# Two stacked transformer blocks in one kernel: the order of work around the last stick-breaking units of block one

## What is computed

```python
def hybrid_layer(x, ...):
    h = rmsnorm(x, g_pre) @ w_in
    (a_q, a_k, a_v, b_b, b_c, b_x, c_q, c_kv, c_kr, d_q, d_k, d_v, gate) = jnp.split(h, SPLIT_IDX, axis=-1)
    ya = swa_sink_attention(...)          # 4 heads, window 128
    yb = short_gated_conv(b_b, b_c, b_x, conv_w, conv_b)
    yc = mla(...)                         # 4 heads, latent attention
    yd = stick_breaking_attention(...)    # 4 heads
    y = jnp.stack([ya, yb, yc, yd], axis=2)
    y = rmsnorm(y, g_grp.reshape(N_GROUPS, GROUP_WIDTH)).reshape(b, s, D_MIX)
    y = y * jax.nn.silu(gate)
    return x + rmsnorm(y @ w_out, g_post)

def stick_breaking_attention(q, k, v):    # per block of 128 queries
    z = q k^T * scale
    log_keep = where(mask, log_sigmoid(-z), 0)
    after = cumsum(log_keep, reverse=True) - log_keep
    a = where(mask, exp(log_sigmoid(z) + after), 0)
    return a @ v
```

## Time and profile before

| quantity | value |
|---|---|
| median of 3 runs | 2416.64 us |
| lowest and highest of them | 2414.21, 2417.61 us |
| the profiled execution's own time | 2422.64 us |
| its span, first to last instruction | 2420.8 us |
| mean granted TensorE clock | 0.982 |
| PE busy | 2270.5 us, 94% |
| DVE busy | 1654.6 us, 68% |
| ACT busy | 1016.5 us, 42% |
| POOL busy | 689.1 us, 28% |

### The profile page before, as it was taken

One profiled execution on the slowest core, in us unless ns is written; L12 is line 12 of the kernel. 1 busy time (PEld: TensorE's weight loads), 2 busy tenths in 40 slices (PEclk: granted clock), 3 DMA queues, 4 the chain that ended last, 5 costly groups with the idle time before them and its releaser, 6 DMA issues.

```text
span 2420.8 us, 34619 instructions
## 1 busy us (share of the span) xinstructions
PE 2270.5 (94%) x11722; PEld 1782.6 (74%) x11722; DVE 1654.6 (68%) x2744; ACT 1016.5 (42%) x1665; POOL 689.1 (28%) x418
## 2 busy tenths in 40 slices
PE   8999899999798799989998999999999989999998
PEld 5766466766477589976766788888768667888886
DVE  8776578775588667645687476676566865766765
ACT  4344623345534356544253444442242634444421
POOL 3211033211132156642100333334321013333342
PEclk9999899999899899999999999999999999999999
DMA  5421234422243145543210234436531102444464
GB/s 211 169 79 59 76 110 144 156 70 70 61 156 114 35 146 183 176 152 117 79 36 1 96 131 139 155 132 226 187 132 53 36 4 93 145 150 145 140 236 140
DMA packets 81102, 286.88 MB, mean 119 GB/s; under 512 B 9009, under 2 KB 11218, under 8 KB 80564
## 3 DMA queue, kind: packets, MB, share of 16 engines
q1 hardware_dynamic: 80948, 284.95, 34.5%
HBM read 282.82 MB, written 2.10 MB: 118 GB/s over the span
## 4 chain that ended last, share of the span: by engine, by line
PE 49%; DVE 3%; issue 1%; ACT 1%; DVEq 0%; ACTq 0%
PE banks L1174 6%; PE banks L1168 6%; PE banks L1172 6%; PE banks L1191 3%; PE banks L1190 3%; PE banks L1197 3%; PE banks L887 3%; PE banks L888 3%; PE banks L892 3%; PE banks L1046 2%; PE banks L1065 2%; PE banks L1076 2%; PE banks L909 1%; PE banks L904 1%; PE banks L905 1%
## 5 line engine op out<-in xcount | busy, mean ns | idle before, releaser
L1497 ACT ACTIVATE wh_t<-ring 128x1024 fp32r<-128x1024 f32 x264 | 279.0, 1058 | 496.6 <-PE banks L1174 297.9
L1977 DVE TENSOR_TENSOR wl_t<-ring,wh_t 128x512 fp32r<-128x512 f32 x264 | 202.8, 769 | 285.0 <-ACT wh_t L1497 280.2
L2333 POOL TENSOR_TENSOR wl_t<-ring,wh_t 128x512 fp32r<-128x512 f32 x132 | 223.5, 1696 | 486.4 <-ACT wh_t L1497 464.9
L2365 POOL TENSOR_TENSOR wl_t<-ring,wh_t 128x512 fp32r<-128x512 f32 x132 | 236.6, 1793 | 419.8 <-ACT wh_t L1497 419.7
L2300 POOL TENSOR_TENSOR wl_t<-ring,wh_t 128x512 fp32r<-128x512 f32 x72 | 119.6, 1664 | 460.7 <-ACT wh_t L1255 444.6
L1168 PE MATMUL banks<-xh_t,wh_t 128*128 128x512 f32 (+1 forms) x960 | 203.0, 354 | 0.0
L1174 PE MATMUL banks<-xl_t,wh_t 128*128 128x512 f32 (+1 forms) x960 | 203.0, 354 | 0.0
L1172 PE MATMUL banks<-xh_t,wl_t 128*128 128x512 f32 (+1 forms) x960 | 203.0, 354 | 0.0
L1190 PE MATMUL banks<-gh_t,wh_t 128*128 128x512 f32 (+1 forms) x528 | 180.6, 354 | 1.0 <-ACT wh_t L1497 1.0
L1191 PE MATMUL banks<-gl_t,wh_t 128*128 128x512 f32 (+1 forms) x528 | 180.3, 354 | 0.0
L1168 PEld LDWEIGHTS banks<-xh_t,wh_t 128*128 128x128 f32 x960 | 161.4, 189 | 25.0
(11 more groups left out here) (388 smaller groups left out, 4583.5 us busy)
## 6 DMA issues: line engine op xcount, KB each, us to landing
ring<-w_d SPq DMA_DIRECT2D x338, 512.0 KB, 4.0
m_t<-wmod_d SPq DMA_DIRECT2D x160, 512.0 KB, 3.5
qh_t<-tables_d SPq DMA_DIRECT2D x6, 512.0 KB, 4.6
m_t<-tables_d SPq DMA_DIRECT2D x6, 512.0 KB, 5.4
par<-p_d SPq DMA_DIRECT2D x4, 696.0 KB, 6.5
x_t<-x_in_d SPq DMA_DIRECT2D x4, 512.0 KB, 6.3
big<-tables_d SPq DMA_DIRECT2D x2, 1024.0 KB
out_d<-x_t SPq DMA_DIRECT2D x4, 512.0 KB, 2.8
```

Source lines behind the costliest of these rows:

```text
L1497: nc.scalar.activation(WH[j % 2], slot2(j), ACT.Copy).then_inc(sm2["w2_hi"], 1)
L1977: nc.vector.tensor_tensor(WL[j % 2][:, 512:1024], slot2(j)[:, 512:1024], WH[j % 2][:, 512:1024].bitcast(F32), ALU.subtract).then_inc(sm2[" ...
L2333: pool.tensor_tensor(WL[j % 2][:, 0:512], slot2(j)[:, 0:512], WH[j % 2][:, 0:512].bitcast(F32), ALU.subtract).then_inc(sm2["w2_lo_a"], 1)
L2365: pool.tensor_tensor(WL[q % 2][:, 0:512], slot2(24 + q)[:, 0:512], WH[q % 2][:, 0:512].bitcast(F32), ALU.subtract).then_inc(sm2["w2_lo_a"], 1)
```

## The change

Three steps move, on three engines; nothing is added or removed. PE: in iteration 7 `z_scores(7)` goes ahead of the first `high_pair`. ACT: the sigmoids of gate chunks 5 to 7 go from the end of iteration 5 to iteration 7, behind unit 7's logarithm chain and ahead of unit 6's closing exponential; `y_high` of chunks 2 and 3 goes from iteration 7 to iteration 6, right behind chunks 0 and 1. DVE: `take(27)` and `w_low(29)` go behind unit 6's softplus.

```diff
@@ PE
                 for u in range(1, len(U) + 1):
                     if pieces:
                         piece()
+                    if u < len(U):
+                        z_scores(u)
                     if u == 7:
                         acc_begin(28)
                         acc_begin(29)
...
                         high_pair(range(2))
                     elif u == 8:
                         high_pair(range(2, 4))
-                    if u < len(U):
-                        z_scores(u)
                     if u in (2, 3, 4):
                         group_sum(u - 2)
@@ ACT
                     if u >= 1:
                         hp, k = U[u - 1]
+                        if u == 7:
+                            gate_sigmoids(range(5, KD))
                         act.wait_ge(*at("wz_ready", u))
...
                     if u == 2:
                         gate_sigmoids(range(5))
-                    elif u == 5:
-                        gate_sigmoids(range(5, KD))
                     elif u == 6:
-                        y_high(0)
-                        y_high(1)
+                        for c in range(4):
+                            y_high(c)
                     elif u == 7:
-                        y_high(2)
-                        y_high(3)
                         group_square(3, (0,))
@@ DVE
                 for u in range(len(U)):
-                    if u in (2, 4, 6):
+                    if u in (2, 4):
                         j = 24 + u // 2
                         take(j, H[GATE + j - 20])
                         w_low(j + 2)
...
                     elif u == 6:
+                        take(27, H[GATE + 7])
+                        w_low(29)
                         stick_copy(0)
                     modulation(16 + u)
```

## The result

| kernel | median of its runs | lowest to highest |
|---|---|---|
| before | 2415.43 us (4 runs) | 2414.0 to 2417.61 |
| changed | 2401.36 us (4 runs) | 2400.45 to 2406.11 |

The ratio is 0.9946, with a 95% interval of 0.993 to 0.9961: 14.1 us less by the medians, where 19.8 were forecast. The interval stands for 9.4 to 16.9 us, so the direction was right and the forecast gain was too large; the time lies inside the stated range of 2392 to 2404. The profiled execution of the changed kernel took 2406.11 us, 16.5 less than that of the kernel before.

A forecast was written before the change was run, and what follows sets the result against it. PE, busy 94% of the span, bounds the kernel. Per layer 4.25, 1.62, 2.59 and 1.42 us make about 9.9; twice that, 19.8, off the median 2416.64 gives 2396.8 us, range 2392 to 2404.

The forecast's parts named there:

- What bounds the kernel: Whole kernel: PE, busy 94% of the span, bounds it; only PE's waits or its clock can pay.
- ACT's order as the cause: Ahead of the first pair: sigmoids and table loads delay unit 6's chain and `y_high`; without them `y_high(0)` comes 6.17 us earlier.
- The dates: Layer 0: unit 7's scores at about 281.6, first pair at 284.15, `stick_values(1)` at about 299.2 against 309.14.
- The second wait: PE's idle time ahead of the output product's second pair in each layer, claimed to vanish: 1.42 us.
- What moves behind it: ACT's sigmoids and table loads, DVE's gate steps (ending at 295.6) and SP's loads come later or move, at no cost.
- the moved copy set the date: DVE's copy of tile 27 and `w_low(29)`, 0.87 us later than before, end the first pair's wait at 284.15.
- The step that failed: First pair of the output product runs at full clock, 2.06 us instead of 3.68, saving 1.62 a layer.
- rival 2: Clock still falls around the first pair, costing 1.6 to 3 us a layer: 2400 to 2403 us, chance 0.15.
- Rival 1: POOL's chunk 2 subtraction goes before `w_low(29)`, delaying low weights 1.27 us: first pair at 285.4, 2399.4 us, chance 0.22.
- Rival 3: An unseen wait keeps unit 6's chain or unit 7's scores where they were: 2413 to 2417 us, chance 0.03.
- rival 4: Clock falls between 280.8 and 284.15 and stays at half until `stick_values(1)`: slower, 2427 us, chance 0.02.
- The better half of rival 2: Half-clock stretch at 324 goes, or first pair starts at 283.1: 1.0 to 1.7 us more a layer, 2393 to 2395, chance 0.08.

The follow-up runs named there:

- e6: Changed kernel with DVE's copy of tile 27 and low part of weight tile 29 moved ahead of the gate products of chunks 2 and 3: 2396.16 us.
- e3: Changed kernel with the DVE part undone, copy of tile 27 and low part of weight tile 29 again ahead of unit 6's softplus: 2401.65 us.
- e4: Changed kernel with two filler matmuls in each of PE's two short gaps, ahead of unit 7's scores and ahead of the first pair: 2400.59 us.
- e7: Changed kernel with modulation rows 24 and 25 moved into DVE's idle time ahead of unit 7's closing exponential, products to unused SBUF: 2402.95 us.
- e5: Changed kernel run and profiled once more without any edit, beside the kernel before: 2400.47 us, ratio 0.992.
- e8: Changed kernel with the early copy, modulation rows 24 and 25 aside, and two filler matmuls ahead of unit 7's scores: 2395.04 us, ratio 0.9902.
- e10: Changed kernel with the early copy and two filler matmuls ahead of unit 7's scores, modulation rows where they were: 2394.05 us, ratio 0.9896.

## Why the prediction was right, and where it was off

*What bounds the kernel* and *ACT's order as the cause* were right: e1 moves ACT's rows alone and gets 13.4 of the 17.4 us in the two stretches, e2 moves PE's alone and gets nothing that can be measured.

*The dates* came as worked out. On the forecast's clock (0.76 less) unit 7's scores started at 281.62 (forecast 281.6), the first pair at 284.18 (284.15), released by DVE's `w_low` as named. The second wait vanished. *What moves behind it* cost nothing, as said: the sigmoids and table loads end while unit 6's sums run, DVE's tail ends at 294.4 on that clock (forecast 295.6). That the moved copy set the date was right (e6). What it cost was not: put back in front it costs as much (e3).

*The step that failed* is the clock. The sum took the first pair at full speed, 3.68 - 2.06 = 1.62 us a layer, and had everything behind run at full clock. The pair took 3.53, so that term brought 0.15, and `stick_values(1)` came at 300.45 on that clock instead of 299.2. This is rival 2 at its cheaper end, with its 2400 to 2403 us, to which the prediction gave a chance of 0.15 against the 0.50 of the forecast. At full clock the stretch comes out as summed: L is 19.69 to 19.73 in both layers of e4 and e7 and 19.68 in layer 1 of e5, 0.25 under the forecast. The second error was to subtract a saving read in an execution of 2422.64 us from a median that lies 6 us lower. The text noted the distance and did not ask what it was. It was in the main half-clock time, part of it in the very stretch: L of before is 29.90 and 29.82 in one profile, 28.36 and 28.59 in the other, so 2.8 of the 19.8 us were not there to be saved in an execution like the second. Over both layers the stretch takes 59.72 or 56.95 us in the two profiles of before and 42.36 or 40.78 in the two of the changed kernel: the same edit saves 14.6 to 18.9 us there, depending on which two are compared. The 14.1 us of the medians hold other differences too, such as the 1.5 us lost at 480 to 484, and no run splits them.

*Rival 1*, POOL winning the turn, did not happen: `w_low(29)` started at 284.16, just as POOL's first subtraction ended (in a narrower view POOL's second starts at 284.17), and took 0.68; POOL's second took 1.81. With dates 0.02 us apart the turn was a toss, and it fell DVE's way. *Rival 3 and rival 4* did not happen.

The better half of rival 2 named the half-clock stretch at 324 to 328 going away, for 1.0 to 1.7 us more a layer. It did go, and brought 0.85 us in layer 1 and nothing in layer 0. Not foreseen were the waits for DVE that appear under it at full clock.

Still open: what makes one pass through a gap keep the full clock and another fall, even within one execution (e5). With the early copy, and so with at most one such gap, all six passes of e6, e8 and e10 stayed at full clock; that fits the gaps as the cause, and is no proof. No run changes the clock alone. Nor was the DVE part tried alone on the kernel before: there ACT's third sigmoid would wait for the copy, the copy for the softplus and the softplus for ACT.

## What to carry to other kernels

When a profiled execution lies off the median of the runs, look first at its mean granted clock, and size every term that rests on half-speed rows for both cases; what an idle gap costs in clock is not a constant of the kernel. Where a layer is run twice, read both passes before calling a number the kernel's. When a VectorE subtraction with two SBUF inputs sets a date beside GpSimd's, try it well ahead of that date: here both orders around GpSimd's instruction cost the same, and the early place gained although GpSimd slowed the subtraction there too. Work moved into an engine's idle time helps only if the next item's data can also be there; otherwise the wait moves on with its queue.

## What the runs showed of the hardware

- The same kernel before gave executions near 2414.5 us (clock 0.986) and near 2423 us (0.982) on one chip, interleaved: 8 us, more than half of the effect under study. Two profiles of it, at 2422.64 and 2411.76 us, have the same waits in the stretch (7.63, 1.42, 1.19).
- Gaps of 0.86 and 1.06 us with 1.5 us of small matmuls between (0.87 and 0.97 in e3) were followed by half clock in five passes (both layers of the changed kernel and of e3, layer 0 of e5) and by full clock in three (layer 1 of e5, both layers of e7).
- A subtraction of 0.68 us on VectorE became 1.46 us when GpSimd's had started 0.37 us ahead of it. The softplus, with one input in PSUM, was not lengthened: in e3 it starts at 284.93 while GpSimd's second subtraction (284.42, 1.74 us) runs, and takes 0.94.
- Of two such instructions that want to start together, the order decides who pays: GpSimd first by 0.07 us, VectorE's takes 2.31 us for 1.23 (changed kernel, 324.18); VectorE first by 0.15 us, GpSimd's takes 2.22 for 1.29 (e5, 323.51).
